# Wider spacing of projection chunks, half-width products in the inverse, and a later start of the gates in a hybrid attention and expert kernel

## The reference, cut to what matters

```python
m = jnp.where(strict_lower, jnp.einsum("bhncd,bhnsd->bhncs", k_beta, k) * decay, 0.0)
t_inv = lax.linalg.triangular_solve(eye + m, eye, left_side=True, lower=True, unit_diagonal=True)
...
mix = jax.nn.sigmoid(gate_sb) * (o_sb @ w_sb_out) + jax.nn.sigmoid(gate_dn) * (o_dn @ w_dn_out)
h = h + mix @ w_o
...
s1, i1 = lax.top_k(s[:, :, 0], PEER_TOPK)
s2, i2 = lax.top_k(s[:, :, 1], PEER_TOPK)
top_s, pos = lax.top_k(cand_s, PEER_TOPK)          # cand_s: sums of the two halves
gate = jax.nn.softmax(top_s, axis=-1)
u = u_tab[ib]
act = jax.nn.gelu(jnp.einsum("td,ted->te", xb, u), approximate=False)
return jnp.einsum("te,ted->td", act * gb, v_tab[ib])
```

## Time and profile before

| | |
|---|---|
| time, median of 3 runs | 2072.38 us (2068.15 to 2075.09) |
| time of the profiled execution | 2077.68 us |
| its span, first to last instruction | 2076.0 us |
| mean granted TensorE clock | 0.984 of full speed |
| TensorE matmul busy | 1957.6 us (94%) |
| TensorE weight load busy | 1745.3 us (84%) |
| VectorE busy | 1395.0 us (67%) |
| ScalarE busy | 815.2 us (39%) |
| GpSimd busy | 652.7 us (31%) |

### The profile page before, as it was taken

One profiled execution on the slowest core, in us unless ns is written; L12 is line 12 of the kernel. 1 busy time (PEld: TensorE's weight loads), 2 busy tenths in 40 slices (PEclk: granted clock), 3 DMA queues, 4 the chain that ended last, 5 costly groups with the idle time before them and its releaser, 6 DMA issues. The chain is left out here.

```text
span 2076.0 us, 30528 instructions
## 1 busy us (share of the span) xinstructions
PE 1957.6 (94%) x11569; PEld 1745.3 (84%) x11569; DVE 1395.0 (67%) x2676; ACT 815.2 (39%) x1260; POOL 652.7 (31%) x682
## 2 busy tenths in 40 slices
PE   7999999999997899998998989999989999999999
PEld 7776676677665678898998979999989999999999
DVE  5543543533632654299899998888767787777777
ACT  4333433433432543242433346565533333333332
POOL 4133033033031100059987832222212222222221
PEclk9999999999999899999999999999999999999999
DMA  3210210210200742249998968888779999999997
GB/s 115 77 51 21 65 41 13 72 36 21 82 16 11 254 134 82 84 149 343 311 330 270 308 196 298 312 311 305 266 251 318 320 312 328 319 320 319 317 317 241
DMA packets 147986, 411.79 MB, mean 198 GB/s; under 512 B 15616, under 2 KB 63872, under 8 KB 147328
## 3 DMA queue, kind: packets, MB, share of 16 engines
q1 hardware_dynamic: 109056, 269.31, 37.5%
q0 software_dynamic: 38784, 140.53, 20.7%
HBM read 360.23 MB, written 49.55 MB: 197 GB/s over the span
## 5 line engine op out<-in xcount | busy, mean ns | idle before, releaser
L1404 ACT ACTIVATE expert_hi<-raw 128x1024 fp32r<-128x1024 f32 x288 | 305.3, 1061 | 422.8 <-PE psE L86 404.3
L84 PE MATMUL psE<-x2h,expert_hi 128*128 128x384 f32 x1024 | 350.9, 343 | 13.6 <-POOL expert_lo L1523 13.6
L1559 DVE TENSOR_TENSOR expert_lo<-raw,expert_hi 128x1024 fp32r<-128x1024 f32 x215 | 262.9, 1224 | 149.6 <-ACT expert_hi L1404 148.7
L84 PE MATMUL psE<-w_hi,expert_hi 128*128 128x384 f32 x1024 | 350.8, 343 | 10.5 <-DVE expert_lo L1559 5.6
L86 PE MATMUL psE<-x2h,expert_lo 128*128 128x384 f32 x1024 | 345.8, 338 | 0.0
L85 PE MATMUL psE<-x2l,expert_hi 128*128 128x384 f32 x1024 | 345.7, 338 | 0.0
L86 PE MATMUL psE<-w_hi,expert_lo 128*128 128x384 f32 x1024 | 343.9, 336 | 0.0
L85 PE MATMUL psE<-w_lo,expert_hi 128*128 128x384 f32 x1024 | 343.9, 336 | 0.0
L1517 POOL DMA_INDIRECT few_gathered<-in_peer_v,picked_expert x128 | 133.5, 1043 | 429.4 <-DVE few_y L1750 388.5
L1517 POOL DMA_INDIRECT few_gathered<-in_peer_u_rows,picked_expert x128 | 149.5, 1168 | 264.6 <-DVE few_gathered L1743 239.5
L1523 POOL TENSOR_TENSOR expert_lo<-raw,expert_hi 128x1024 fp32r<-128x1024 f32 x73 | 184.7, 2530 | 133.1 <-ACT expert_hi L1404 131.2
(11 more groups left out here) (295 smaller groups left out, 3516.9 us busy)
## 6 DMA issues: line engine op xcount, KB each, us to landing
raw<-in_peer_u SPq DMA_DIRECT2D x128, 512.0 KB, 4.7
raw<-in_peer_v SPq DMA_DIRECT2D x128, 512.0 KB, 6.7
expert_acts<-gelu SPq DMA_DIRECT2D x124, 192.0 KB, 5.4
gelu<-expert_acts SPq DMA_DIRECT2D x124, 192.0 KB, 3.9
expert_gates<-shared SPq DMA_DIRECT2D x4, 4096.0 KB, 16.2
gates_in<-expert_gates SPq DMA_DIRECT2D x32, 512.0 KB, 6.3
ring<-in_w_xonly SPq DMA_DIRECT2D x24, 512.0 KB, 3.3
ring<-in_w_full SPq DMA_DIRECT2D x16, 512.0 KB, 3.9
```

What stands on the lines that cost most here:

```text
L84: nc.tensor.matmul(out, sh, mh, start=first, stop=False)
L1404: nc.scalar.activation(wh[:, s % R, :], raw[:, s % R, :], ACT.Copy).then_inc(S["hi_done"], 1)
L1559: v.tensor_tensor(wl[:, s % R, :], raw[:, s % R, :], wh[:, s % R, :].bitcast(F32), ALU.subtract).then_inc(S["lo_done"], 1)
```

## The change: four parts

1. **Planner.** At the unit and level points a chunk may start only when the former chunk of its bank ended at least 5 points earlier, in place of 2. Elsewhere the distance stays. In pairs 0 to 2 this moves steps of three chunks: the 20 steps at the unit and level points become 16, and the 8 steps in the chain become 12 (wt keeps 4, start to inverse0 keep theirs). Steps at level 1, in unit 20 and one of the two at level 6 fall away. Pair 3 keeps its plan.
2. **Half columns.** The two products of the inverse run over half of their moving columns (those that this level changes), 64 in place of 128, read in runs of 2 to the power a. VectorE updates the two parts apart: two instructions of 128 columns in place of one of 512 (last levels: one of 128 in place of 256).
3. **First gathers spread.** GpSimd makes the `low` of chunks 13 and 14 before it waits for the first tile's picks, and that of 15 before the first gather. The six gathers in a row become two after each `low` until the quota is reached; the quota is 2 higher and runs over 62 chunks in place of 60.
4. **Gates later, last dots later.** The last `turn` stands behind chunk 74 (73 before), the first gates behind chunk 75 (73 before). The last 4 of the first 128 dots (LATE_DOTS) use slots 2 to 5, and so are gathered after the last gates. GpSimd makes `low` up to chunk 77 (75 before); behind the last one-hot operands, seven dots fall between two `low` instead of four.

```diff
-                if k == 0 and ended[before] + 2 > at and not (name == "end" and ended[before] + 1 == at):
+                if k == 0 and ended[before] + (5 if name[0] in ("unit", "level") else 2) > at and not (name == "end" and ended[before] + 1 == at):
...
+        def half_cols(ap, a, odd):
...
+            lead = " ".join("pqr"[:len(ap.shape) - 1])
+            ap = ap.rearrange(f"{lead} (k two b) -> {lead} k two b", two=2, b=1 << a)
+            return ap[:, :, odd, :] if len(lead) == 1 else ap[:, :, :, odd, :]
...
-                            part = xx[0:r, n, :, w0:, 0:r]
-                            inc(nc.vector.tensor_tensor(part, part, bank[0:r, 3 if t % 2 else 5, 0:4 * r].rearrange(
-                                "p (e w c) -> p e w c", e=2, w=2)[:, :, w0:, :], ALU.subtract), "x_updated")
+                            for w in range(w0, 2):
+                                part = half_cols(xx[0:r, n, :, w, 0:r], a, w)
+                                last = nc.vector.tensor_tensor(part, part, bank[
+                                    0:r, 3 if t % 2 else 5, w * r:(w + 1) * r].rearrange(
+                                        "p (e k b) -> p e k b", e=2, b=1 << a), ALU.subtract)
+                            inc(last, "x_updated")
...
+                                blocks = lambda w: bank[0:r, b, (2 * w + e) * r // 2:(2 * w + e + 1) * r // 2].rearrange(
+                                    "p (k b) -> p k b", b=1 << a)
                                 if not last_level(a, n):
-                                    mm(bank[0:r, b, 2 * e * r:(2 * e + 1) * r], xx[0:r, n, e, 1, 0:r],
-                                       ys[0:r, n, e, 0:r], start=True, stop=True)
-                                last = mm(bank[0:r, b, (2 * e + 1) * r:(2 * e + 2) * r], ys[0:r, n, e, 0:r],
-                                          xx[0:r, n, e, 1, 0:r], start=True, stop=True)
+                                    mm(blocks(0), xx[0:r, n, e, 1, 0:r], half_cols(ys[0:r, n, e, 0:r], a, 0), start=True,
+                                       stop=True)
+                                last = mm(blocks(1), ys[0:r, n, e, 0:r], half_cols(xx[0:r, n, e, 1, 0:r], a, 1), start=True,
+                                          stop=True)
...
+LATE_DOTS = 4
...
-ROUTED_AT = (13, 33, 53, 73)
+ROUTED_AT = (13, 33, 53, 74)
...
-PAIRS_A = ROUTED_AT[-1]
+PAIRS_A = ROUTED_AT[-1] + 1
...
-            r = n % (2 + R) if n < ROUTE_DOTS else (n - ROUTE_DOTS) % 2 if n < FIRST_DOTS else 2 + (n - FIRST_DOTS) % R
+            r = n % (2 + R) if n < ROUTE_DOTS else 2 + (n - FIRST_DOTS) % R
+            if ROUTE_DOTS <= n < FIRST_DOTS - LATE_DOTS:
+                r = (n - ROUTE_DOTS) % 2
...
-            for j in range(3, ROUTED_AT[0]):
+            for j in range(3, ROUTED_AT[0] + 2):
                 low(U + j)
             pool.wait_ge(S["few_picked"], 2)
-            for n in range(2 + R):
-                gather(n)
-            sent = 2 + R
-            for j in range(ROUTED_AT[0], PAIRS_A + 3):
+            sent = 0
+            for j in range(ROUTED_AT[0] + 2, PAIRS_A + 3):
                 low(U + j)
-                while sent < min(R + (j + 1 - ROUTED_AT[0]) * ROUTE_DOTS // (PAIRS_A - ROUTED_AT[0]), ROUTE_DOTS):
+                while sent < min(2 + R + (j + 1 - ROUTED_AT[0]) * ROUTE_DOTS // (PAIRS_A - ROUTED_AT[0]),
+                                 2 * (j - 1 - ROUTED_AT[0]), ROUTE_DOTS):
                     gather(sent)
                     sent += 1
-            for n in range(ROUTE_DOTS, FIRST_DOTS):
+            for n in range(sent, FIRST_DOTS - LATE_DOTS):
                 gather(n)
             pool.wait_ge(S["gates_made"], 2 * PAIRS_B)
-            for n in range(FIRST_DOTS, 2 * HK):
+            for n in range(FIRST_DOTS - LATE_DOTS, 2 * HK):
                 gather(n)
```

## The result

The changed kernel takes 2087.16 us (median of 20 runs, 2076.12 to 2097.47), the kernel before, run beside it, 2076.24 us. The ratio is 1.0045, interval [1.0029, 1.0061]. The forecast was 2052. (It was worked out from a median of 2072.38, of the three runs known then; 20 runs of the same kernel have 2076.24.) The profiled execution of the changed kernel took 2095.67 us, at a mean granted clock of 0.969; the one before took 2077.68 at 0.984. Over all runs the mean clock is 0.974, against 0.983 to 0.984 before.

A forecast was written before the change was run, and what follows sets the result against it. TensorE's waits were taken as the bound, VectorE second in the routing. Spacing -2.0, half columns -0.5, routing and gates -12.5, U to V -3.5, clock -1.0 and -0.6 sum to -20.1: forecast 2052 us, range 2039 to 2066.

The forecast's parts named there:

- What bounds the kernel: Whole kernel: TensorE busy 92 to 98% of every stage, so its waits count; VectorE second bound, in the routing alone.
- Spacing, -2.0: Front half: nine TensorE waits (9.4 us) go, partly given back at levels 1 and 6 and unit 20; -2.0 us.
- Half columns, -0.5: Inverse products and updates in the front half: -0.5 us at the end of units and copies, bounds 0 and -3.
- On TensorE I take nothing: Inverse products: weight loading sets the pace at 64 or 128 moving columns, so 0 us, bounds 0 and -9.
- rivals 3 and 4: Half products faster on TensorE, 2030 to 2042 (0.12); VectorE's short-run updates set the pace, slower (0.04, with unseen causes).
- Routing and gates, -12.5: Back half, up to the first gates: picks earlier, two more chunks done before the gates; -12.5 us.
- The picks are then ready at 1213.75 - 11.5 + 7.0 = 1209.3.: End of VectorE's routing: 11.5 us of waits for gathered rows become 7.0, so the last tile is picked at 1209.3.
- Rival 1: Routing gives the gain back: TensorE waits near chunks 25 to 31 and 52; 2058 to 2068, chance 0.22 shared with another.
- U to V, -3.5: TensorE's gap between U and V: 5.62 us becomes 1.8 to 2.1 through later last dots; -3.5 us.
- G: End of the last gates, from which `low` of chunk 127 was timed at G+12.5 and TensorE's restart at G+22.6.
- Clock terms, -1.0 and -0.6: Less slow clock behind the gaps before the gates (-1.0 us) and behind the U to V gap (-0.6 us).

The follow-up runs named there:

- old_quota: The kernel before with only the later gates and last dots, its gather quota left as before (over 60 chunks, not 62): ratio 0.9942 [0.9922, 0.9962].

## Why the prediction was wrong

**What bounds the kernel** was right for TensorE and too narrow for VectorE. It was seen as busy 316.30 of 331.30 us, and its work was then taken as fixed: "From 931.7 it works 282 us, of which it waits 11.5." 45.0 of these were instructions held up by GpSimd.

**Spacing, -2.0.** Right in its steps: the nine waits are gone, and 1.36 us at level 1 (1.25 forecast) and 0.68 in unit 20 (0.6) stand in their place; the 0.6 forecast at level 6 did not come. Alone it measures 0.9982, -3.7 us, which cannot be told from -2 or 0.

**Half columns, -0.5.** The step that failed is "On TensorE I take nothing". The pace was right (0.11 us an instruction at either width), and VectorE's 284 ns for 128 columns too (about 290 forecast), so rivals 3 and 4 fell with their mechanisms. But the price was looked for in durations at the full clock; what the products do to the clock stood in no term and no rival. With the spacing it was 12.8 us.

**Routing and gates, -12.5.** The failed step: "The picks are then ready at 1213.75 - 11.5 + 7.0 = 1209.3." The waits came out nearly as said (8.0 for 7.0), the sum did not, since it took VectorE's work as fixed. The picks came at 1223.1, 13.8 late: 10.9 are longer work of VectorE within the routing, 1.9 the later first picks, 1.0 the waits. Rival 1 named TensorE's waits near chunks 25 to 31 and 52, and they came, but not this. The two chunks laid into the gap before the gates were right: 8.3 us, kept in old_quota.

**U to V, -3.5.** Mis-sized: 5.62 became 4.52, -1.1. From the last gates on:

```profile
1514.18 1.22 DVE L1758 SCALAR_TENSOR_TENSOR few_gathered<-few_gathered,psE 128x1024 f32<-128x1024 f32 x1 [1.26 <-issue]
...
1515.32 3.49 DVE L1574 TENSOR_TENSOR expert_lo<-raw,expert_hi 128x1024 fp32r<-128x1024 f32 x3
1524.42 0.43 DVE L1797 TENSOR_TENSOR gelu<-gelu,gates_in 128x256 f32<-128x256 f32 x1 [5.61 <-issue]
```

With G at 1501.5, `low` of chunk 127 is the first of the three and ends at G+15.0, not G+12.5: the rounds over two slots still waited 1.95 and 2.33 us for rows. From the load to the restart it took 10.3 us, not 9.6. And what was gained before V was not kept in this profile: V took 3.8 us longer.

**Clock terms, -1.0 and -0.6.** The sign was right: from 880 to 1530 us the time at the lower level went from 38 to 29 us. The front's 50 us more outweighed it.

## What to carry to other kernels

Before an engine's idle time is filled, look at what its neighbour does in that time: here two lows laid into a wait of GpSimd of 9.34 us made one step of VectorE take 4.38 us in place of 2.29. When the work of two such engines is laid anew, what they cost each other changes with it, even if neither has more to do: 29 to 57 us in one routing, by the kernel. Sort the instructions of the bounding engine by duration within one shape; a shape that takes now 0.29 and now 3.0 us is held up by someone, and work that seems fixed is not. And where TensorE streams short products, read the granted clock beside the pace: an edit that takes columns out without taking time out can pay with the clock, and the payment may show only with a second edit.

## What the hardware showed that was not expected

- TensorE's clock fell to 1.2 GHz while it was busy 2.80 of 2.80 us, in products of 64 moving columns; with 128 at the same pace, behind the same wait of 0.68 us, it stayed at 2.4.
- Issuing a gather takes GpSimd 2.82 us in place of 0.94 beside a long VectorE instruction (at 986.45 of the kernel before, beside line 1707), so the hold works both ways.
- A `low` on 1024 columns costs GpSimd 2.41 us, but VectorE up to 2.8 for each of its instructions that meets it: 45.0 us over the routing of the kernel before, 16% of it.
